# Three weight tiles of a hybrid decoder layer's input projection move from the first stage into the second

## What is computed

```
proj = rms_norm(x, norm1) @ w_in
sb_q, sb_k, sb_v, dn_qkv, dn_z, dn_a, dn_b, hg_q, hg_f, hg_i, hg_g = split(proj)

# A) stick-breaking attention, 4 heads x 64, strictly causal:
z = (q @ k.T) / 8
A[t,s] = sigmoid(z[t,s]) * prod over s<j<t of (1 - sigmoid(z[t,j]))
sb_o = rms_norm(A @ v, sb_gain)

# B) gated DeltaNet, 4 heads x 128: short causal conv and silu on dn_qkv, then a chunked
#    recurrence (chunks of 128 tokens here) with a triangular inverse per chunk
# C) HGRN2, 4 heads, 64x64 state: a gated linear recurrence
x = x + concat(sb_o, dn_o, hg_o) @ w_out
out = rms_norm(x + swiglu(rms_norm(x, norm2)), final_norm)
```

## Time and profile before

| what | value |
|---|---|
| median of 3 runs | 1454.74 us (1454.07 to 1455.75) |
| the profiled execution's own time | 1452.92 us |
| its span, first to last instruction | 1450.9 us |
| PE, VectorE, ScalarE, GpSimd busy | 97%, 51%, 37%, 43% |
| first stage, second stage, start of the third | to 102 us, 102 to 443 us, from 443 us |

### The profile page before, as it was taken

One profiled execution on the slowest core, in us unless ns is written; L12 is line 12 of the kernel. 1 busy time (PEld: TensorE's weight loads), 2 busy tenths in 40 slices (PEclk: granted clock), 3 DMA queues, 4 the chain that ended last, 5 costly groups with the idle time before them and its releaser, 6 DMA issues.

```text
span 1450.9 us, 24660 instructions
## 1 busy us (share of the span) xinstructions
PE 1402.0 (97%) x9457; PEld 1176.1 (81%) x9457; DVE 739.9 (51%) x1288; ACT 542.8 (37%) x1293; POOL 618.7 (43%) x552
## 2 busy tenths in 40 slices
PE   5999999999997999999999999999999999999997
PEld 4777888879786888888887788888888888888886
DVE  5005547363563688876147843533535335354436
ACT  6224445444433444542233423223232232332435
POOL 3214233142424566661302946346354463543650
PEclk9999999999997999999999999999999999999999
DMA  5122323232225322524210022120121211302103
GB/s 176 52 79 74 93 68 112 84 112 71 70 65 139 102 83 72 159 78 150 59 29 1 29 59 63 54 59 35 53 80 36 59 52 35 87 30 59 59 30 130
DMA packets 122004, 106.52 MB, mean 73 GB/s; under 512 B 6353, under 2 KB 107297, under 8 KB 121889
## 3 DMA queue, kind: packets, MB, share of 16 engines
q1 hardware_dynamic: 121744, 104.43, 23.9%
q10 hardware_dynamic: 144, 0.52, 0.1%
HBM read 83.95 MB, written 20.99 MB: 72 GB/s over the span
## 4 chain that ended last, share of the span: by engine, by line
PE 90%; DVE 4%; POOL 3%; issue 2%; ACT 1%; DVEq 0%; POOLq 0%; ACTq 0%
PE banks L2113 9%; PE banks L2115 9%; PE banks L2114 9%; PE banks L318 6%; PE banks L320 6%; PE banks L319 6%; PE banks L2130 5%; PE banks L2132 5%; PE banks L2131 5%; PE banks L652 2%; PE banks L654 2%; PE banks L653 2%; PE banks L1899 2%; PE banks L1900 2%; PE banks L1901 2%
## 5 line engine op out<-in xcount | busy, mean ns | idle before, releaser
L2237 POOL TENSOR_TENSOR w_l<-area,w_h 128x512 fp32r<-128x512 f32 x102 | 143.5, 1413 | 195.7 <-ACT w_h L2150 195.7
L2237 POOL TENSOR_TENSOR w_l<-w_raw,w_h 128x512 fp32r<-128x512 f32 x86 | 118.3, 1379 | 165.3 <-ACT w_h L2150 165.3
L2381 DVE TENSOR_TENSOR area<-area,banks 128x512 f32<-128x512 f32 x176 | 121.1, 688 | 120.6 <-PE banks L2132 118.2
L318 PE MATMUL banks<-act_h,w_h 128*128 128x512 f32 x352 | 140.5, 399 | 0.0
L320 PE MATMUL banks<-act_h,w_l 128*128 128x512 f32 x352 | 137.4, 390 | 0.0
L319 PE MATMUL banks<-act_l,w_h 128*128 128x512 f32 x352 | 137.2, 390 | 0.0
L306 POOL TENSOR_TENSOR w_l<-w_raw,w_h 128x1024 fp32r<-128x1024 f32 x24 | 59.4, 2477 | 154.9 <-ACT w_h L299 137.7
L2113 PE MATMUL banks<-act_h,w_h 128*128 128x512 f32 x320 | 124.5, 389 | 0.0
L2114 PE MATMUL banks<-act_l,w_h 128*128 128x512 f32 x320 | 124.5, 389 | 0.0
L2130 PE MATMUL banks<-w_h,ff_h 128*128 128x512 f32 x320 | 124.5, 389 | 0.0
L2131 PE MATMUL banks<-w_l,ff_h 128*128 128x512 f32 x320 | 124.5, 389 | 0.0
(11 more groups left out here) (301 smaller groups left out, 3321.5 us busy)
## 6 DMA issues: line engine op xcount, KB each, us to landing
w_raw<-in_w_in SPq DMA_DIRECT2D x22, 512.0 KB, 4.1
area<-in_x SPq DMA_DIRECT2D x8, 1024.0 KB, 7.9
projected_tm<-area SPq DMA_DIRECT2D x32, 256.0 KB, 2.6
w_raw<-in_w_gate SPq DMA_DIRECT2D x12, 512.0 KB, 4.6
area<-in_w_down SPq DMA_DIRECT2D x12, 512.0 KB, 3.9
w_raw<-in_w_up SPq DMA_DIRECT2D x12, 512.0 KB, 4.6
projected_cm<-area SPq DMA_DIRECT2D x20, 256.0 KB, 2.1
area<-projected_tm SPq DMA_DIRECT2D x8, 640.0 KB, 5.5
```

The lines of the kernel that those rows point to most:

```text
L318: e.matmul(dst, w_h[:, b, k], act_h[:, k, cols], start=(k == 0), stop=False)
L2237: e.tensor_tensor(slot(w_l, u), raw_use(u), slot(w_h, u).bitcast(F32), ALU.subtract).then_inc(sems["fl"], 1)
L2381: e.tensor_tensor(dst, dst, bank(4 + (16 * p + c) % 4), ALU.add).then_inc(sems["x_added"], 1)
```

## The change

Only the tiles of head pair 0 (query, key, value) stay in the first stage: it now has tiles 0 to 3. The tiles of head pair 1 become six new projection units at the head of the second stage (`LEADS`, LEAD = 6), so that there are 54 projection units (ND = 54) beside 48 attention units, and attention unit k stands beside projection unit k, of which unit k - 6 was there before. Projection units 48 to 53 have no attention unit beside them. The value tile of head pair 0 is transposed after the first projection unit (`first_values`, 8 transposes) and copied in VectorE's step 1 (`first_values_taken`); the value tile of head pair 1 goes through the path of the conv tiles' transposes (`turn`, `stage_tok`, 8 transposes). The waits for the values stand at their first use (`weigh` 0 and 24), those for query and key of pair 1 at `scores` 24. The last two groups of row units change places ("gate" is third, "plain" last). The table of which tile is split at which step (`next_split`) becomes `SPLITS`, with the same steps relative to a tile's first use.

```diff
-    ROWS = [("swish", C_Z, Z_AT), ("swish", C_Z + HGW, Z_AT + HGW), ("plain", C_HI, I_AT), ("gate", C_HG, G_AT)]
+    ROWS = [("swish", C_Z, Z_AT), ("swish", C_Z + HGW, Z_AT + HGW), ("gate", C_HG, G_AT), ("plain", C_HI, I_AT)]
...
-    NH = RUN * len(ROWS)
-    W_AB, W_P1, W_OUT = 0, 7, 7 + 2 * NS
-    D_OUT = 2 * W_P1 + NH
+    LEADS = ("query", "key", "value")
+    LEAD = 2 * len(LEADS)
+    NH, ND = 12 * SBH, LEAD + RUN * len(ROWS)
+    W_AB, W_P1 = 0, 4
+    W_OUT = W_P1 + len(LEADS) + 2 * NS
+    D_OUT = 2 * W_P1 + ND
...
-            return w_in[:, :, C_AB:C_AB + NAB] if w == W_AB else in_tile(w - 1)
+            return w_in[:, :, C_AB:C_AB + NAB] if w == W_AB else in_tile(2 * w - 2)
...
-            for v in range(2):
-                for th in range(2):
-                    n = 2 * v + th
-                    e.wait_ge(sems["dense_evac"], FIRST_AT[5 + v, 1] + 1)
-                    e.wait_ge(sems["small_ready"], n + 1)
-                    e.wait_ge(sems["decay_dve"], 8)
-                    for j in range(4):
-                        mm = e.transpose(bank(2 + n % 2)[:, j * P:(j + 1) * P],
-                                         sb_t[:, 4 + v, (4 * th + j) * P:(4 * th + j + 1) * P], ident[:, :])
-                    mm.then_inc(sems["small_turned"], 1)
+
+        def first_values(e):
+            e.wait_ge(sems["dense_evac"], FIRST_AT[3, 1] + 1)
+            for th in range(2):
+                for j in range(4):
+                    mm = e.transpose(bank(6 + th)[:, j * P:(j + 1) * P], sb_t[:, 4, (4 * th + j) * P:(4 * th + j + 1) * P], ident[:, :])
+                mm.then_inc(sems["small_turned"], 1)
...
             def turn(k):
                 reach(e, "tm_ready", before(STAGED, k))
                 reach(e, "q_sq", before(IS_Q, k))
-                reach(e, "act_ready", before(GATED, k + 1))
+                if KINDS[k] == "value":
+                    e.wait_ge(sems["small_ready"], 4)
+                    mix_taken(e, k)
+                    src = sb_t[:, 5, (1 - k % 2) * HALF:(2 - k % 2) * HALF]
...
-            for k in range(NH + 5):
-                if k < NH:
-                    if k % 2 == 0:
-                        scores(k)
+            for k in range(ND + 2):
+                if k < NH and k % 2 == 0:
+                    scores(k)
+                if k < ND:
                     mix_free(e, k, k % 2)
                     if BY_ROWS[k]:
                         dense_rows(e, k, bank(k % 2))
                     else:
-                        dense_half(e, W_P1 + SLOT[k], (W_P1 + SLOT[k]) % 2, k % 2, bank(k % 2))
+                        w = W_SLOT0 + SLOT[k]
+                        dense_half(e, w, w % 2, k % 2, bank(k % 2))
+                if k == 0:
+                    first_values(e)
                 if 1 <= k <= NH:
                     turn_weights(k - 1)
...
             def take_dense(k):
...
+                if k < LEAD:
+                    tile, half = 2 * (k // 2) + 1, k % 2
+                    if k < 2:
+                        dst = sb_t[:, tile, half * HALF:(half + 1) * HALF]
+                    else:
+                        dst = sb_t[:, tile, (1 - half) * HALF:(2 - half) * HALF][:, ::-1]
+                    e.activation(dst, bank(k % 2), ACT.Copy).then_inc(sems[f"mix_evac{k % 2}"], 1)
                     return
```

More of the change, by code:

```diff
@@ L74, in trunk_program @@
     BY_DVE = [kind in ("swish", "swish_chan") for kind in KINDS]
-    CHANNEL = [(NC // 2) * (SLOT[k] // NS) + (SLOTS[SLOT[k] % NS][1] - C_DN) // P if CONV[k] else -1 for k in range(NH)]
+    CHANNEL = [(NC // 2) * (SLOT[k] // NS) + (SLOTS[SLOT[k] % NS][1] - C_DN) // P if CONV[k] else -1 for k in range(ND)]
     IS_Q = [0 <= ch < DNH for ch in CHANNEL]
@@ L78, in trunk_program @@
     IS_F = [kind == "chan" for kind in KINDS]
-    TURNED = CONV
+    TURNED = [kind in ("conv", "value") for kind in KINDS]
     STAGED = [t and not q for t, q in zip(TURNED, IS_Q)]
-    TOKM = [t or r for t, r in zip(STAGED, BY_ROWS)]
-    WHOLE = [not (t or r) for t, r in zip(TURNED, BY_ROWS)]
-    SLOT_END = [max(k for k in range(NH) if SLOT[k] == m and not BY_ROWS[k]) for m in range(2 * NS)]
+    STORED = [c and not q for c, q in zip(CONV, IS_Q)]
+    TOKM = [t or r for t, r in zip(STORED, BY_ROWS)]
+    WHOLE = [kind in ("swish_chan", "chan") for kind in KINDS]
+    TILE_AT = {W_SLOT0 + SLOT[k]: k - 1 for k in range(ND) if not BY_ROWS[k] and k % 2 == 1}
+    SPLITS = {TILE_AT[w - 1] if TILE_AT[w] == TILE_AT[w - 1] + 2 else TILE_AT[w] - NR_RUN: w for w in range(W_P1 + 1, W_OUT)}
     ENDS = [hh == 1 and at + n == (q + 1) * P for hp, q, hh, at, n in UNITS]
@@ L296, in split_high @@
                 last = 2 * (w - 1) + (1 if w == 2 else 0)
-                reach(e, "dense_done", 2 * W_P1 + SLOT_END[w - W_P1 - 2] + 1 if w >= W_P1 + 2 else last)
+                reach(e, "dense_done", 2 * W_P1 + TILE_AT[w - 2] + 2 if w >= W_P1 + 2 else last)
             cols = slice(0, NAB if w == W_AB else P)
@@ L518, in first_dve, with first_values_taken @@
             decay_dve(e)
[L519 to L524, removed]
+        def first_values_taken(e):
+            for th in range(2):
+                e.wait_ge(sems["small_turned"], th + 3)
+                e.tensor_copy(v_tm[:, 4 * th:4 * th + 4, 0:P], bank(6 + th).rearrange("p (t c) -> p t c", c=P)).then_inc(sems["small_ready"], 1)
         def decay_dve(e):
@@ L657, in trunk_program @@
         ROWS_SPLIT = (3, 5)
[L659 to L663, removed]
         def mix_tile(w):
-            i, (kind, col, per, at) = (w - W_P1) // NS, SLOTS[(w - W_P1) % NS]
+            if w < W_SLOT0:
+                return in_tile(2 * (w - W_P1) + 1)
+            i, (kind, col, per, at) = (w - W_SLOT0) // NS, SLOTS[(w - W_SLOT0) % NS]
             return w_in[:, :, ds(per * i + col, P)]
@@ L729, in store_rows @@
             def store_rows(k):
-                kind, col, at = ROWS[k // RUN]
-                first = 2 * (k % RUN - NC_RUN) * P
+                kind, col, at = ROWS[RUN_OF[k]]
+                first = 2 * (IN_RUN[k] - NC_RUN) * P
                 if GATED[k]:
@@ L906, in key_squares @@
                 ins.then_inc(sems["k_sq"], 1)
-            for k in range(NH + 5):
-                if 1 <= k <= NH:
+            for k in range(ND + 4):
+                if 1 <= k <= ND:
                     take_dense(k - 1)
@@ L958, in left_after @@
                 e.tensor_tensor(att[:, k % 2, 0:n], take[:, k % 2, 0:n], rem[:, hh, at:at + n], ALU.mult).then_inc(sems["a_ready"], 1)
-            for k in range(NH):
-                if k % 2 == 0 and next_split(k):
-                    split_low(e, next_split(k), next_split(k) % 2)
-                if k % RUN in ROWS_SPLIT:
-                    rows_low(e, k // RUN, ROWS_SPLIT.index(k % RUN))
-                left_after(k)
+            for k in range(ND):
+                if k in SPLITS:
+                    split_low(e, SPLITS[k], SPLITS[k] % 2)
+                if IN_RUN[k] in ROWS_SPLIT:
+                    rows_low(e, RUN_OF[k], ROWS_SPLIT.index(IN_RUN[k]))
+                if k < NH:
+                    left_after(k)
         def mix_dve(e):
@@ L1014, in stage_tok @@
                 reach(e, "k_sq", before(IS_K, k - 1))
+                if KINDS[k] == "value":
+                    first = 4 * (1 - k % 2)
+                    e.tensor_copy(v_tm[:, first:first + 4, P:2 * P], TURN.rearrange("p (j c) -> p j c", c=P)).then_inc(sems["tm_ready"], 1)
+                    return
                 e.tensor_copy(tm_stage[:, k % 2], TURN.rearrange("p (j c) -> p j c", c=P)).then_inc(sems["tm_ready"], 1)
@@ L1028, in stage_out @@
                 e.tensor_copy(o_stage[:, u % 2], O[u % 2][:, P:2 * P]).then_inc(sems["o_evac"], 1)
-            for k in range(NH + 6):
+            for k in range(ND + 3):
                 if 3 <= k < NH + 3 and ENDS[k - 3]:
```

120 lines of the change are left out of this document (69 added, 51 removed).

## The result

| | before | changed |
|---|---|---|
| median | 1454.72 us (4 runs, 1454.07 to 1455.75) | 1468.44 us (4 runs, 1467.72 to 1468.81) |
| profiled execution | 1452.92 us, span 1450.9 | 1468.09 us, span 1466.1 |

A forecast was written before the change was run, and what follows sets the result against it. PE, busy 1402.0 of 1450.9 us, was taken as the bound, leaving idle time and clock. Seams 1.2 + 0.2 = 1.4 us, other terms 0: 1451.5 for the profiled execution, 1453.3 us with the median's 1.8 offset; range 1450.3 to 1456.2.

The forecast's parts named there:

- the sum holds seams alone: Whole kernel: matmuls, copies and splits keep their shapes and only change places, so only the seams count: 1.4 us won.
- SP's queue and the HGRN2 chain: SP's loads around the second seam: L1111 not late, nothing waits for the first row weights; no gain or loss.
- First seam: End of first stage, 102 to 106 us: PE's waits of 0.4 and 0.78 us go; 1.2 us won, bounds 1.1 to 1.5.
- Second seam: 443 to 453 us: table load 3.53 us sooner, last projection matmul 3.3 later; 0.2 us won, bounds -0.1 to 0.5.
- Inside the second stage: Attention beside conv work shifts by six units, with no PE wait to lose: 0 us, bounds 0 and -0.6.
- rival C: Second stage: conv steps late under attention, PE waits at eight key and value tiles; 5.0 us slower, 1458.3 us, chance 0.08.
- The clock: Behind the second seam: falls to half within 2 us of the same place in the work; 0 us, bounds -1.5 to 1.5.
- A: Second seam: PE's 4.5 us of idle time really won, beside the first seam's 1.2; 1449.0 us, chance 0.08.
- B: Inverse of chunk 0, behind the second seam: the clock stays up, 7.5 us won; 1445.8 us, chance 0.04.

The follow-up runs named there:

- experiment 1: Changed kernel with the loads of tiles 4 and 5 put back ahead of SP's wait for the decay chain: 1453.33 us, ratio 0.9989 to the kernel before.
- experiment 6: experiment 1 plus ScalarE's table load and the lengths moved ahead of the last two row units' copies: 1450.19 us, ratio 0.9968.
- experiments 7 to 9: experiment 6 plus one, three and two thrown-away matmuls at each place in the inverse of chunk 0: 1451.55, 1447.58 and 1445.94 us.
- experiment 2: Kernel before with only the loads of tiles 4, 5 and 6 moved behind SP's decay-chain wait and twelve gain loads: 1471.19 us, ratio 1.0113.
- experiment 4: Changed kernel with tile 4's load alone ahead of SP's decay-chain wait, tile 5's left behind the gain loads: 1457.24 us, ratio 1.0023.
- experiment 3: Changed kernel with tile 4's load between the decay store and the twelve gain loads: 1458.59 us, ratio 1.0024.
- experiment 5: Changed kernel with the twelve gain loads behind tiles 4 to 6 and the first row weights, decay-chain wait left ahead: 1457.71 us, ratio 1.0024.

## Why the prediction was wrong

**The step that failed** is the premise of the sum, that all matmuls, copies and splits are still there and that "the sum holds seams alone": the loads are not in that list, and stand in the sum at nothing without a reason. The part "SP's queue and the HGRN2 chain" looked at SP only at the second seam and at the first load of row weights, and did not ask where the loads of tiles 4 to 6 would stand. The cut of `first_sync` from tiles 2 to 6 to tiles 2 and 3 moves three loads past the wait for the decay chain and the twelve gain loads, and tile 4 is the next that PE needs. The runs showed 13.3 us of wait for it and 1.9 us at half clock in place of that nothing, 15.2 us.

Most of the price could have been read from the kernel before: the decay store is issued at 64.52 us and the last gain loads end at about 70.5. With the 4.1 us from issue to landing that its page gives for tile loads and 3.6 us for ScalarE and POOL (84.15 - 80.53, of the changed kernel), tile 4 is ready at 78.2 us or later, for a PE that wants it at 71. That is an estimate of 7 us of wait, and a fallen clock. The 5.5 us by which the load behind the gain loads is slower stand in no row of the kernel before that I read.

**First seam, 1.2 us.** The two waits are gone; what that gave by itself was not run. **Second seam, 0.2 us.** ScalarE's part held to a few hundredths: 0.61 us to the table load and 6.39 us from the last copy to the transposes, where it had been 9.92, so 3.53 us less. PE's part did not. The last row copy starts at 443.43 us before and at 446.45 in experiment 1; less the 0.34 us by which that execution began its full projections later (30.34 against 30.00) it is 2.7 us later, where 3.3 - 1.2 = 2.1 were forecast. So at L1324 (L1291 before) the two seams together had won 3.53 - 2.68 = 0.85 us and not 1.4. Which of them gave less than its share is open.

**Inside the second stage, 0**: held; neither the changed kernel nor experiment 1 has a wait of PE between 100 us and the seam, so rival C did not occur. **The clock, 0**: it fell again, but the stretch was longer. From the mean of 0.71 over 452 to 454 us and 0.96 over 480 to 482 it was at half from about 452.8 to 480.2 us in experiment 1, 27.3 us, against 454.5 to 478.4, 23.9 us, before. The start and the end of that stretch of work in experiment 1, PE in time:

```profile
452.84 1.12 PE L1324 MATMUL banks<-ident,area 64*64 64x64 f32 x16 [3.67 <-DVE area L1675]
...
477.88 1.91 PE L1299 MATMUL banks<-area 128*128 128x128 f32 x8
...
480.98 1.16 PE L1203 MATMUL banks<-area 128*128 128x128 f32 x8
```

and the same products in the kernel before:

```profile
478.39 1.06 PE L1266 MATMUL banks<-area 128*128 128x128 f32 x8
...
480.46 1.16 PE L1170 MATMUL banks<-area 128*128 128x128 f32 x8
```

At L1324 the execution of experiment 1 stands 0.51 us ahead of the one before (452.84 against 453.35), at L1203 it is 0.52 us behind it. That is one execution of each. So the agreement of the medians, 1.3 us against 1.4, is in part luck: the seams gave less than worked out, and the clock differed as well. For the idle time that I had not seen the clock's term was missed by 1.9 us.

**The rivals.** A fell: PE's idle time there is ScalarE's chain (experiment 6). B did not occur by itself, but experiments 7 to 9 show its price, 7.5 us as stated. The rival that came true, a load that starves PE, was not among them: the slower side had been sought on VectorE alone. The range was too narrow since its terms held only engines' work, not the queue. It was also added up wrongly, without consequence here: the bounds of the terms give 2.1 us to the faster side and 2.5 to the slower (1451.2 to 1455.8), and half way from there to A and C lie 1450.1 and about 1457, not 1450.3 and 1456.2.

## What to carry to other kernels

When a loop over loads is cut short, the loads that leave it do not stay where they were: list the queue's instructions in order, mark each wait in it, and check for every load that crosses one when it will be issued against when it is needed. Small loads that every partition reads were not free here to what stood behind them in the queue: put them where the next large load is not urgent. And idle time at a seam belongs to the chain that ends last; moving the work of the engine that waits won less than 1 us here, moving the chain 3.1.

## What the runs showed of the hardware

- A 512 KB tile load issued directly behind twelve gain loads of 32 to 64 KB (each a row of DRAM spread over 128 partitions) was taken by ScalarE 9.4, 9.5, 9.7 and 10.5 us after its issue (changed kernel, experiments 2, 4 and 3), against 3.9 where it stood ahead of them (experiments 3 and 5), also with a second tile directly behind it.
- Nine matmuls of 512 columns behind an idle stretch of 13.3 us took 3.96 us, where nine take 2.05 later. Behind a wait of 2.1 us the clock fell in one profiled execution (experiment 5) and not in another (experiment 3).
- A chain of small matmuls, with PE busy 19.1 of 25 us, ran at a mean clock of 0.55; with two thrown-away matmuls of 512 columns in each gap PE was busy 24.2 us at 1.00, and the kernel was faster for doing more work (1445.94 against 1450.19 us, ratios 0.9944 and 0.9968 in two sessions). With one in each gap the clock was held in four of ten executions. The Trainium skill (TensorE: Matmul & The Clock Gate, "What's actually happening") says that activity releases the throttle; the runs agree, with 1.00 against 0.55.
